# Transposing the attention weights by a product with a diagonal matrix, in the second block of a two-block float32 layer on one core

## The chip, the core and the metric

The kernel runs on one core of a Trainium2 chip. TensorE (PE in the profile) multiplies matrices into PSUM; VectorE (DVE), ScalarE (ACT) and GpSimd (POOL) do the rest of the arithmetic; SyncE (SP) issues most transfers. Each engine works through its own instructions in order and waits on semaphores for the others. The metric is the device time of one execution in microseconds (us), as a median over executions.

## What is computed

The reference runs two blocks on a sequence of 1024 positions of width 1024, all in float32. The first holds a sliding-window attention, an mLSTM, a cross attention and a feed-forward part. The second holds an RWKV-7 recurrence (512 columns) beside a banded attention (8 heads of 64), and an output projection. The change is in the banded attention of the second block:

```python
def chunk_band_attention(q, k, v, q_g, k_g, rel_bias):
    ...
    s = jnp.einsum('bhnqd,bhnkd->bhnqk', qc, kb).astype(jnp.float32) * (HEAD_DIM ** -0.5)
    ...
    s = s + bias[None, :, None]
    s = jnp.where(valid[None, None, :, None, :], s, -1e30)
    p = jax.nn.softmax(s, axis=-1).astype(v.dtype)
    o = jnp.einsum('bhnqk,bhnkd->bhnqd', p, vb)
```

Chunks have 64 rows and see 576 keys (8 chunks to the left and their own). The softmax of each row divides its exponentials by their sum; that division is what the change moves.

## The kernel before

Five programs, one for each engine, are written from one list of steps (class `Order`). Most of the list is made by a planner: `flow` (L666) holds several streams of steps, keeps a clock for each engine, and always takes the next step of the stream that can go on soonest. What a step costs on each engine it reads from the table in `work` (the rows of `band_*` stand at L566 to L576). So a changed cost can change the order in which the engines meet their instructions, and every engine keeps to its order at run time.

The stage around the change begins when the projections of the second block are done, some 2045 us into the span. Four kinds of work run side by side in it:

- preparation of the recurrence's inputs (`prep_*`) for the second half of the sequence, with the row sums at L1898,
- for each of 8 pairs of chunks, the triangular inverse and products of the recurrence (`pre_*`, at L1916 to L2011 on TensorE), a chain of small products in which each level waits for VectorE's copy of the level before (L2808 to L2884),
- the recurrence itself (`seq_*`, L2011 to L2073),
- the banded attention, in units `(j, n)`: a pair of heads j (4 of them) and 128 rows n (8 of them). 32 units run in three lanes (`lane`, L1258), each unit through `band` (L1221).

A unit goes through these steps, for both its heads (a = 0, 1), over W = 128 min(5, n + 1) keys, so that the units with n = 4 to 7, half of them, have the full W = 640:

1. `band_s`: scores, TensorE (L1857); VectorE adds the bias, writes the scores to the buffer `m.Pv3[p]` and takes the maximum (L2699).
2. `band_x`: ScalarE takes the exponential in place, with the row sums as an accumulated output (L3271).
3. `band_p`: VectorE takes the reciprocal of the two columns of sums (L2706), and multiplies each head's 128 x W weights in place by its column (L2710).
4. `band_t`: TensorE transposes the weights, 128 x 128 at a time, by the unit matrix (L1511, the helper `transpose`, which all transposes of the kernel share); ScalarE copies the result out of PSUM (L3279).
5. `band_o`: TensorE multiplies the values by the transposed weights (L1878); `band_y` on VectorE multiplies by the gate (L2716).

When all units with n < 4 and the recurrence are done, the mark "most" lets SyncE fetch what the output projection needs; ScalarE and VectorE split the operand (`fin_part`, L3359 and L2929), then the projection runs on TensorE (`mm`, L1525 to L1527) while the last units end between its products. `mm` splits each float32 product into three products of reduced precision.

The cross attention of the first block (`cross_t`, `cross_o`) is untouched, and is of use for comparison: `cross_t` transposes through the same helper (L1511), and `cross_o` (L1811) is a plain float32 product of 128 x 128 by 128 x 128.

Of the kernel before, what the change touches and what calls it, by code (L numbers as in the profile page):

```python
# [4 lines left out]

F32 = mybir.dt.float32
F32R = mybir.dt.float32r
TOTAL = 52736
ALU = mybir.AluOpType
ACT = mybir.ActivationFunctionType  # L10
AX = mybir.AxisListType
MUL, ADD, SUB, MAX, MIN = ALU.mult, ALU.add, ALU.subtract, ALU.max, ALU.min
# [34 lines left out]
X0 = NCOLS + NROWS + NCST + 32 + NSMALL  # L47
PIECES = [X0, 8192, 2048 * NSLOT, 16384, (TOTAL - X0 - 32768) // 16 * 16]
G0 = X0 + 8192
# [4 lines left out]
class Signals:  # L54
# [12 lines left out]
    def on(self, name, *event, by=1):  # L67
        self.n[name] = self.n.get(name, 0) + by
        assert self.value.setdefault((name, *event), self.n[name]) == self.n[name], (name, event)
        return self.sem(name), by  # L70
# [5 lines left out]
    def at(self, name, *event):  # L76
        assert not self.strict or (name, *event) in self.value, (name, event)
        return self.sem(name), self.value.get((name, *event), 1)
# [58 lines left out]
def v3(ap, k):  # L137
    return ap.rearrange("p (k n) -> p k n", k=k)
# [32 lines left out]
class Memory:  # L171
# [40 lines left out]
    def work(self, a, n):  # L212
        return self.f32(W0 + a, n)
# [18 lines left out]
    def pair(self, b):  # L232
        return self.PS[:, 1024 * b:1024 * b + 1024]
# [27 lines left out]

    def first(self):
        work, f32, small = self.work, self.f32, self.small
        self.xh = [[f32(X0 + 4096 * h + 512 * k, 512) for k in range(8)] for h in range(2)]
        self.xs = [[self.XT[:, k, 512 * h:512 * h + 512] for k in range(8)] for h in range(2)]
        self.aqT, self.akT = v3(work(8192, 4096), 4), work(12288, 1024)
        self.avt = v3(work(13312, 1024), 8)
        self.avf = [work(13312 + 512, 512), work(31784, 512)]
        self.mqk = [work(14336 + 1024 * m, 1024) for m in range(8)]
# [57 lines left out]
    def second(self):  # L327
        work, f32, small = self.work, self.f32, self.small
# [17 lines left out]
        self.pads_s = [work(30720, 513), work(31233, 513)]  # L346
        self.lo, self.hsq = work(31746, 512), work(32258, 512)
        self.mun = small[:, 512:529]
        self.PLc, self.bon = v3(small[:, 544:608], 4), v3(small[:, 608:672], 8)
        m2 = self.m2  # L350
        self.mAR = v3(m2[:, 0:128], 2).unsqueeze(2).to_broadcast([128, 2, 4, 64])
# [207 lines left out]
def work(step):  # L559
# [7 lines left out]
        wide = min(5, x[1] + 1) / 5  # L567
        return [("pe", 1.1 * wide + 0.1), ("v", 1.7 * wide + 0.1)]
    if name == "band_p":
        return [("v", 0.2 + 1.5 * min(5, x[1] + 1) / 5)]  # L570
    if name == "band_x":
        return [("a", 0.2 + 0.85 * min(5, x[1] + 1) / 5)]
    if name == "band_t":
        return [("pe", 0.1 + 0.55 * min(5, x[1] + 1) / 5), ("a", 0.2 + 0.6 * min(5, x[1] + 1) / 5)]
    if name == "band_o":
        return [("pe", 0.1 + 1.1 * min(5, x[1] + 1) / 5)]  # L576
    if name == "rms_out":
# [50 lines left out]
class Order:  # L628
# [206 lines left out]
    def window(self, n, jp):  # L835
        u = 2 * n + jp
        yield from self.after("ha", *[("ws", u - 1)] * (u > 0), ("avt", n // 4))
        yield from self.room((self.pairs, 1), (self.P, 1))
        self.done.add(("ws", u))
        b, free = self.pairs.take()  # L840
        p, pfree = self.P.take()
        st = self.stat()
# [8 lines left out]
        b, free = self.pairs.take()  # L851
        self.P.give(p, ("win.pe", "t", n, jp))
        q, qfree = self.PT.take()
# [92 lines left out]
    def opened(self):  # L946
        ha = ("upto", "pe", "ha")
        for i in range(3):
            self.P.give(i, ha)
        for i in range(2):  # L950
# [9 lines left out]
    def cross(self, n):  # L960
        if n:
            yield from self.after(("cs", n - 1))
        yield from self.after("kv", f"q{n // 4}")
        yield from self.room((self.pairs, 1), (self.P, 1))
        self.done.add(("cs", n))
        b, free = self.pairs.take()
        p, pfree = self.P.take()
        st = self.stat()
# [536 lines left out]
def tensor_program(pe, w, m, S, o):  # L1505

    on, at, bank, pair, cs = S.on, S.at, m.bank, m.pair, m.cs

    def transpose(out, in_):
        n = in_.shape[0]  # L1510
        return pe.transpose(out, in_, m.I[0:n, 0:n])  # L1511
# [349 lines left out]
    def band_t(j, n, a, b, free, p, q, qfree):  # L1861
        w.wait_ge(*at("band.v", "p", j, n, a))
        for e in S.each(free):
            w.wait_ge(*e)
        for kt in range(min(5, n + 1)):
            i = transpose(pair(b)[:, kt * 128:(kt + 1) * 128], m.Pv3[p][:, kt * 128:(kt + 1) * 128])
        i.then_inc(*on("band.pe", "t", j, n, a))

    def band_o(j, n, b, q):
# [220 lines left out]
def vector_program(v, w, m, S, o):  # L2090

    on, at, bank, pair, small = S.on, S.at, m.bank, m.pair, m.small
# [373 lines left out]
    def stats(st, G):  # L2466
        return [small[:, 128 + 32 * st + k * G:128 + 32 * st + (k + 1) * G] for k in range(4)]
# [233 lines left out]
                                   op0=ADD, op1=MIN, accum_out=nm[:, a:a + 1]).then_inc(*on("band.v", "max", j, n, a))  # L2701

    def band_p(j, n, p, st):
        W, sm = 128 * min(5, n + 1), stats(st, 2)[2]
        w.wait_ge(*at("band.a", "x", j, n, 1))
        v.reciprocal(sm, sm).then_inc(*on("band.v", "rcp", j, n))  # L2706
        w.wait_ge(*at("band.v", "rcp", j, n))
        for a in range(2):
            P = m.Pv3[p[a]][:, 0:W]
            v.tensor_scalar(P, P, sm[:, a:a + 1], None, MUL).then_inc(*on("band.v", "p", j, n, a))  # L2710

    def band_y(j, n, b):
        sl = slice(n * 128, (n + 1) * 128)
# [1038 lines left out]
```

## Times and profile before

| What | us |
|---|---|
| median of 3 runs | 2424.62 |
| lowest and highest run | 2422.2 and 2427.26 |
| the profiled execution | 2418.48 |
| its span, first to last instruction | 2416.6 |
| PE busy, share of the span | 2277.8, 94% |
| DVE busy, share of the span | 1456.7, 60% |
| ACT busy, share of the span | 937.6, 39% |
| mean granted clock of TensorE, 1 being 2.4 GHz | 0.972 |

Busy time is the time in which an engine had at least one instruction under way. Matmuls are pipelined, so one of 0.27 us can start 0.11 us after the one before; what a row of matmuls costs is read from the length of a run of them, not from the mean of one. "PEld" is TensorE's loading of weights, which overlaps the products. Idle time is put down to the instruction whose semaphore ended it. The profiled execution ran 6.1 us faster than the median of the runs.

### The profile page before, as it was taken

Reading aid. Unit: us, or ns where it says so; the run is one execution under the profiler, and the core shown is the slowest. Engines: PE = TensorE matmul, PEld = TensorE weight load, DVE = VectorE, ACT = ScalarE, POOL = GpSimd, SP = SyncE. Lnnn points to the kernel's source line nnn. Section 1 sums busy time; section 2 is a strip of 40 time slices with the busy share of each in tenths; the row PEclk is TensorE's granted clock in tenths of the full one; section 3 lists DMA queues with packets and bytes.
Section 4 is the critical chain, followed back from the end, with each engine's and each line's share of the span. In section 5 each row is a group of like instructions: output and inputs, shape, how many; then the busy total and the mean of one; then the engine's idle time right before and its main releaser. Section 6 shows DMA issues by size and latency. Waiting matters only on the chain. (4 is left out here: it accounts for less than half of the span.)

```text
span 2416.6 us, 43216 instructions
## 1 busy us (share of the span) xinstructions
PE 2277.8 (94%) x18830; PEld 1848.8 (77%) x18830; DVE 1456.7 (60%) x2456; ACT 937.6 (39%) x1532; POOL 78.7 (3%) x61
## 2 busy tenths in 40 slices
PE   7999988999999999999999999999999998789789
PEld 5777767788888888888878888778777776567667
DVE  5575866565434886777753454646455655767743
ACT  4446432444333443333342433354333232335441
POOL 0000000000000000000000000002000001200000
PEclk9999989999999999999999999989999999799989
DMA  5332252544123232222365534333323113111044
GB/s 179 88 94 66 69 170 71 173 123 129 53 62 119 77 96 83 79 79 86 93 196 164 157 90 135 98 113 110 109 80 107 51 37 97 41 44 44 3 129 150
DMA packets 329349, 238.15 MB, mean 99 GB/s; under 512 B 10948, under 2 KB 288580, under 8 KB 329032
## 3 DMA queue, kind: packets, MB, share of 16 engines
q1 hardware_dynamic: 326424, 229.82, 31.7%
q10 hardware_dynamic: 2736, 5.57, 0.6%
q8 instruction: 148, 2.42, 0.4%
q14 instruction: 41, 0.34, 0.0%
HBM read 202.33 MB, written 33.03 MB: 97 GB/s over the span
## 5 line engine op out<-in xcount | busy, mean ns | idle before, releaser
L1525 PE MATMUL PS<-SR 128*128 128x512 f32 (+2 forms) x1696 | 681.6, 402 | 43.2 <-DVE SR L2106 34.8
L1526 PE MATMUL PS<-SR 128*128 128x512 f32 (+2 forms) x1696 | 659.9, 389 | 0.0
L1527 PE MATMUL PS<-SR 128*128 128x512 f32 (+2 forms) x1696 | 659.7, 389 | 0.0
L2106 DVE TENSOR_TENSOR SR<-SB,SR 128x1024 fp32r<-128x1024 f32 (+1 forms) x240 | 289.1, 1206 | 289.8 <-ACT SR L2967 289.5
L1525 PEld LDWEIGHTS PS<-SR 128*128 128x128 f32 (+1 forms) x1696 | 320.4, 189 | 128.3 <-DVE SR L2106 36.9
L1527 PEld LDWEIGHTS PS<-SR 128*128 128x128 f32 (+1 forms) x1696 | 320.2, 189 | 68.7
L1526 PEld LDWEIGHTS PS<-SR 128*128 128x128 f32 (+1 forms) x1696 | 320.9, 189 | 62.2 <-issue 1.7
L2967 ACT ACTIVATE SR<-SB 128x1024 fp32r<-128x1024 f32 (+1 forms) x240 | 247.5, 1033 | 254.9 <-DMA SB<-in_w_down 116.1
L1546 PE MATMUL PS<-SR 128*128 128x512 f32 x624 | 243.4, 390 | 0.3 <-DVE SR L2232 0.3
L1548 PE MATMUL PS<-SR 128*128 128x512 f32 x624 | 242.8, 389 | 0.0
L1547 PE MATMUL PS<-SR 128*128 128x512 f32 x624 | 242.7, 389 | 0.0
L1546 PEld LDWEIGHTS PS<-SR 128*128 128x128 f32 x624 | 117.1, 188 | 25.1 <-DVE SR L2232 0.7
L1548 PEld LDWEIGHTS PS<-SR 128*128 128x128 f32 x624 | 117.1, 188 | 24.6
L1547 PEld LDWEIGHTS PS<-SR 128*128 128x128 f32 x624 | 117.1, 188 | 24.4 <-issue 0.2
L1511 PE MATMUL PS<-SB 128*128 128x128 f32 (+2 forms) x560 | 87.1, 288 | 31.9 <-DVE SB L2710 13.5
L1511 PEld LDWEIGHTS PS<-SB 128*128 128x128 f32 (+2 forms) x560 | 63.4, 145 | 49.7 <-DVE SB L2710 15.2
L2974 ACT ACTIVATE SB<-PS 128x512 f32<-128x512 f32 (+1 forms) x71 | 39.1, 572 | 151.1 <-PE PS L1527 113.0
L2254 DVE TENSOR_TENSOR SR<-SB,SR 128x1536 fp32r<-128x1536 f32 (+2 forms) x66 | 87.0, 1347 | 0.9 <-ACT SR L3031 0.9
L3031 ACT ACTIVATE SR<-SB 128x1536 fp32r<-128x1536 f32 (+2 forms) x66 | 74.2, 1156 | 20.0 <-DVE SB L2244 18.9
L2142 DVE TENSOR_TENSOR SB<-PS,SB 128x512 f32<-128x512 f32 x48 | 33.2, 691 | 78.7 <-PE PS L1527 78.7
L3279 ACT ACTIVATE SB<-PS 128x640 f32<-128x640 f32 (+4 forms) x64 | 36.4, 569 | 93.7 <-PE PS L1511 93.6
L3065 ACT ACTIVATE SB<-SB 128x1024 f32<-128x1024 f32 x22 | 27.4, 1245 | 116.5 <-DVE SB L2304 116.5
(315 smaller groups left out, 3032.2 us busy)
## 6 DMA issues: line engine op xcount, KB each, us to landing
SB<-in_w_in SPq DMA_DIRECT2D x110, 512.0 KB, 4.0
SB<-in_w_up SPq DMA_DIRECT2D x88, 256.0 KB, 3.3
SB<-in_w_out SPq DMA_DIRECT2D x32, 512.0 KB, 4.2
SB<-in_w_down SPq DMA_DIRECT2D x32, 512.0 KB, 4.1
SB<-in_w_ada SPq DMA_DIRECT2D x12, 1024.0 KB, 5.2
hidden<-SB SPq DMA_DIRECT2D x22, 512.0 KB, 3.4
SB<-hidden SPq DMA_DIRECT2D x43, 256.0 KB, 5.3
asides<-SB SPq DMA_DIRECT2D x36, 256.0 KB, 4.1
```

Source lines behind the costliest of these rows:

```text
L1511: return pe.transpose(out, in_, m.I[0:n, 0:n])
L1525: pe.matmul(out, whi[:, k - k0, :], hi[k], start=(k == 0), stop=False)
L1526: pe.matmul(out, whi[:, k - k0, :], lo[k], start=False, stop=False)
L1527: i = pe.matmul(out, wlo[:, k - k0, :], hi[k], start=False, stop=(k == j.K - 1))
L1546: pe.matmul(out, whi[:, k, :], hi[k], start=first and k == 0, stop=False, skip_group_check=True)
L1547: pe.matmul(out, whi[:, k, :], lo[k], start=False, stop=False, skip_group_check=True)
L1548: x = pe.matmul(out, wlo[:, k, :], hi[k], start=False, stop=(k == 3), skip_group_check=True)
L2106: v.tensor_tensor(m.f32r(a, kn * cn), m.f32(a, kn * cn), m.f32r(a + 1024, kn * cn).bitcast(F32), SUB).then_inc(*on("split.v", p))
L2254: v.tensor_tensor(m.up_unit(m.SR, p, a, 0, b - a), f32_of(p, a, b - a), m.up_unit(m.SR, p, a, 1, b - a).bitcast(F32), SUB).then_inc(*on("u ...
L2967: a.activation(m.f32r(at_ + 1024, kn * cn), m.f32(at_, kn * cn), ACT.Copy).then_inc(*on("split.a", p))
L2974: a.activation(j.dst(t), src, j.func, scale=j.scale).then_inc(*on("gemm.a", "ev", j.name, t))
L3031: a.activation(m.up_unit(m.SR, p, lo, 1, hi - lo), m.up_unit(m.SB, p, lo, 0, hi - lo), ACT.Copy).then_inc(*on("up.a", "hi", p, g))
```

## The change

The reciprocals are no longer multiplied into the weights. `band_p` multiplies the 128 x 128 unit matrix by the column of reciprocals instead, which gives a diagonal matrix D in a new buffer `m.Dv[p]` (one for each of the five buffers `Pv3`). `band_t` then calls a plain matmul with the unnormalized weights as the stationary operand and D as the moving one, so that the product is the transpose of the weights with each column scaled by its row's reciprocal. The steps, waits and signals stay. The costs in `work` follow: `band_p` from up to 1.7 to 0.6 us on VectorE, `band_t` from up to 0.65 to 1.2 us on TensorE. The piece of memory at the end grows to hold D, and the space set aside for dynamic transfers shrinks.

```diff
-TOTAL = 52736
+TOTAL = 57040
+SCRATCH = 1024
...
+        self.Dv = [work(32816 + 128 * i, 128) for i in range(5)]
...
     if name == "band_p":
-        return [("v", 0.2 + 1.5 * min(5, x[1] + 1) / 5)]
+        return [("v", 0.6)]
...
     if name == "band_t":
-        return [("pe", 0.1 + 0.55 * min(5, x[1] + 1) / 5), ("a", 0.2 + 0.6 * min(5, x[1] + 1) / 5)]
+        return [("pe", 0.1 + 1.1 * min(5, x[1] + 1) / 5), ("a", 0.2 + 0.6 * min(5, x[1] + 1) / 5)]
...
         for kt in range(min(5, n + 1)):
-            i = transpose(pair(b)[:, kt * 128:(kt + 1) * 128], m.Pv3[p][:, kt * 128:(kt + 1) * 128])
+            i = pe.matmul(pair(b)[:, kt * 128:(kt + 1) * 128], m.Pv3[p][:, kt * 128:(kt + 1) * 128], m.Dv[p], start=True, stop=True)
         i.then_inc(*on("band.pe", "t", j, n, a))
...
     def band_p(j, n, p, st):
-        W, sm = 128 * min(5, n + 1), stats(st, 2)[2]
+        sm = stats(st, 2)[2]
         w.wait_ge(*at("band.a", "x", j, n, 1))
         v.reciprocal(sm, sm).then_inc(*on("band.v", "rcp", j, n))
         w.wait_ge(*at("band.v", "rcp", j, n))
         for a in range(2):
-            P = m.Pv3[p[a]][:, 0:W]
-            v.tensor_scalar(P, P, sm[:, a:a + 1], None, MUL).then_inc(*on("band.v", "p", j, n, a))
+            v.tensor_scalar(m.Dv[p[a]], m.I, sm[:, a:a + 1], None, MUL).then_inc(*on("band.v", "p", j, n, a))
...
-    nc = _bacc.Bacc("TRN2", target_bir_lowering=False, num_devices=1)
+    nc = _bacc.Bacc("TRN2", target_bir_lowering=False, num_devices=1, dynamic_dma_scratch_size=SCRATCH)
```

Nothing moves before the first unit of the attention, and SyncE's and GpSimd's instructions keep their order throughout. On the other engines the planner's new costs move instructions at two places of interest. (After the change the same code has a line number 2 higher, and 1 higher behind `band_p`.)

VectorE, at the first units with full width. Before, two scalings of 128 x 640 stand between the recurrence's steps L2835, L2841 and L2847:

```order
L2835 TENSOR_TENSOR SB<-SB 128x512
L2706 RECIPROCAL SB<-SB 128x2
L2710 TENSOR_SCALAR SB<-SB 128x640 x2
L2841 TENSOR_TENSOR SB<-SB 128x512
L2716 SCALAR_TENSOR_TENSOR SB<-PS,SB 128x128
L2706 RECIPROCAL SB<-SB 128x2
L2710 TENSOR_SCALAR SB<-SB 128x640 x2
L2847 TENSOR_TENSOR SB<-PS,SB 128x2x128 x2
```

With the change:

```order
L2836 TENSOR_TENSOR SB<-SB 128x512
L2842 TENSOR_TENSOR SB<-SB 128x512
L2848 TENSOR_TENSOR SB<-PS,SB 128x2x128 x2
L2717 SCALAR_TENSOR_TENSOR SB<-PS,SB 128x128
L2708 RECIPROCAL SB<-SB 128x2
L2711 TENSOR_SCALAR SB<-SB 128x128 x2
L2856 TENSOR_TENSOR SB<-PS,SB 128x2x128 x2
```

The scalings are 128 x 128 now, and the recurrence's steps come ahead of them.

TensorE, at the end of the stage, where the output projection (L1525 to L1527) begins. Before:

```order
L1857 MATMUL PS<-SB 128x512 x2
L1857 MATMUL PS<-SB 128x128 x2
L2073 MATMUL PS<-SB 64x64 x16
L1511 MATMUL PS<-SB 128x128 x5
L1525 MATMUL PS<-SR 128x512
L1526 MATMUL PS<-SR 128x512
L1527 MATMUL PS<-SR 128x512
```

With the change, at the same place and then behind 42 products of the projection (a second such pair of rows follows 12 products later):

```order
L1868 MATMUL PS<-SB 128x128 x10
L1880 MATMUL PS<-SB 64x128 x10
L2075 MATMUL PS<-SB 64x64 x16
L1868 MATMUL PS<-SB 128x128 x5
L1527 MATMUL PS<-SR 128x512
L1528 MATMUL PS<-SR 128x512
```

```order
L1529 MATMUL PS<-SR 128x512
L1859 MATMUL PS<-SB 128x512 x2
L1859 MATMUL PS<-SB 128x128 x2
L1527 MATMUL PS<-SR 128x512
L1528 MATMUL PS<-SR 128x512
```

The scores of the last two units have moved from ahead of the projection into it. Four groups of transposes and three of `band_o` stand behind its first product in both.

## Rows read from the trace of the kernel before

**Rows 1.** The page: busy time of the two busiest engines, its share, instructions.
```profile
PE 2277.8 (94%) x18830; PEld 1848.8 (77%) x18830; DVE 1456.7 (60%) x2456; ACT 937.6 (39%) x1532; POOL 78.7 (3%) x61
```

**Rows 2.** Windows of the stage: length, busy times, granted clock, DMA share, GB/s.
```profile
core 0: us, PE busy (x) PEld busy (x) DVE busy (x) ACT busy (x) POOL busy (x), PEclk, DMA share, GB/s
2045.00:2080.00 35.00, 18.77 (x88) 12.44 (x92) 24.53 (x52) 10.17 (x27) 14.51 (x10) 0.50 0.42 143
2080.00:2120.00 40.00, 34.81 (x956) 28.80 (x952) 27.22 (x79) 16.57 (x37) 0.00 (x0) 0.97 0.05 15
2120.00:2160.00 40.00, 33.12 (x820) 25.77 (x810) 27.78 (x76) 17.03 (x40) 4.70 (x4) 0.87 0.13 47
2160.00:2200.00 40.00, 35.01 (x980) 29.26 (x976) 30.17 (x82) 15.57 (x31) 0.97 (x1) 1.00 0.19 66
2200.00:2240.00 40.00, 35.89 (x931) 27.31 (x931) 27.93 (x95) 18.09 (x53) 3.50 (x4) 0.99 0.04 10
2240.00:2280.00 40.00, 34.31 (x843) 27.54 (x840) 31.34 (x83) 16.56 (x31) 4.97 (x4) 0.96 0.01 3
2280.00:2317.00 37.00, 20.07 (x259) 14.89 (x255) 21.89 (x52) 19.91 (x36) 4.46 (x4) 0.78 0.16 41
2317.00:2341.00 24.00, 23.30 (x147) 18.59 (x147) 10.09 (x15) 8.54 (x13) 0.00 (x0) 0.91 0.57 180
sum 296.00, PE 235.29 PEld 184.60 DVE 200.94 ACT 122.44 POOL 33.11; mean PE 29.41 PEld 23.07 DVE 25.12 ACT 15.31 POOL 4.14
```

**Rows 3.** Chain that ended last, 2045 to 2341 us: shares by engine and line.
```profile
by line: PE PS L1857 9.8%; PE PS L1878 9.3%; PE PS L1511 8.7%; DVE SB L2699 5.9%; issue 5.5%; PE PS L1946 5.3%; DVE SB L2710 4.6%; PE PS L1999 2.8%; ACT SB L3279 2.3%; PE PS L1916 2.2%; PE PS L1984 2.2%; PE PS L1525 2.2%; PE PS L1527 1.8%; 
```

**Rows 4.** Waits of PE, 2080 to 2341 us: total us, times, longest.
```profile
PE PS L1525 <- DVE SR L2106: 9.2, 1, 9.2
PE PS L1511 <- DVE SB L2699: 6.1, 8, 2.8
PE PS L1857 <- ACT SB L3279: 5.5, 6, 1.6
PE PS L1511 <- DVE SB L2710: 5.3, 5, 4.1
```

**Rows 5.** Groups by line and shape, 2040 to 2360 us: the transposes of the stage.
```profile
L1511 PE MATMUL PS<-SB 128*128 128x128 f32 x240 | 42.3, 299 | 22.0 <-DVE SB L2710 13.5 <-DVE SB L2699 6.1 <-ACT SB L3279 2.1
```

**Rows 6.** Timeline of the cross attention at full clock: start, length, engine, line.
```profile
626.42 3.73 PE L1811 MATMUL PS<-SB 128*128 128x128 f32 x32
...
629.99 1.04 PE L1511 MATMUL PS<-SB 128*128 128x128 f32 x8
```

**Rows 7.** L2710 alone, windows of the stage, their sum.
```profile
sum 296.00, DVE 31.80; mean DVE 3.98
```

**Rows 8.** Timeline: pairs of L2710, narrow, beside GpSimd's work, and wide.
```profile
2052.26 0.48 DVE L2710 TENSOR_SCALAR SB<-SB 128x128 f32<-128x128 f32 x2
...
2151.54 2.57 DVE L2710 TENSOR_SCALAR SB<-SB 128x512 f32<-128x512 f32 x2
2152.68 1.15 POOL L3401 TENSOR_TENSOR SB<-SB 128x512 f32<-128x512 f32 x1
...
2309.22 1.02 DVE L2710 TENSOR_SCALAR SB<-SB 128x640 f32<-128x640 f32 x2
```

**Rows 9.** Timeline: scores of a full unit at half and at full clock.
```profile
2295.73 2.50 PE L1857 MATMUL PS<-SB 64*128 64x512 f32 x8 [1.65 <-ACT SB L3279]
...
2305.47 1.35 PE L1857 MATMUL PS<-SB 64*128 64x512 f32 x8 [0.79 <-ACT SB L3279]
```

**Rows 10.** Timeline up to the start of the output projection.
```profile
2307.62 0.82 DVE L2699 CUSTOM_DVE_ANT_0 SB<-PS,SB 128x640 f32<-128x640 f32 x1
...
2310.94 4.27 ACT L3359 ACTIVATE SR<-SB 128x512 fp32r<-128x512 f32 x8 [0.86 <-ACT SB L3271]
...
2317.70 0.80 PE L1525 MATMUL PS<-SR 128*128 128x512 f32 x1 [9.17 <-DVE SR L2106]
```

## The prediction

> **What bounds the kernel now.** I read the page first, then the stage of the change in windows, then the chain of waits in it, and last single rows for prices. The page gives TensorE 94% of the span and VectorE 60% [rows 1], but the change touches only the 296 us from 2045 to 2341, so the windows decide. There TensorE is busy for 235.3 us and VectorE for 200.9 [rows 2]; both are loaded. In the 200 us from 2080 to 2280 TensorE is busy for 173.1 us, 87%, and VectorE for 144.4, 72%. In the last 24 us TensorE has next to no gap: the output projection fills it. Only at both ends is it short of work: 18.8 of 35 us before 2080, where VectorE prepares the recurrence, and 20.1 of 37 us from 2280 to 2317, where little is left but attention units that wait for themselves.
>
> The chain of waits says whether these 13% of gaps mean that TensorE is free. It is not: the three largest shares of the chain are the attention's own products, scores 9.8%, values 9.3%, transposes 8.7%, and VectorE's scaling L2710 has 4.6% [rows 3]. TensorE's waits are many and short; after the one for the projection's weights (9.2 us, once) the longest sums are 5 to 6 us each [rows 4]. The engines hand each other a dense chain, and TensorE has the greater part of it.
>
> **The change, part by part.**
>
> *TensorE, transposes become products.* The stage has 240 of them: 30 pieces for each of 8 heads, and 240 records in the group [rows 5], one for each. The price of a transpose: 8 back to back take 1.04 us; less the tail of the last (0.27), that is 0.77 / 7 = 0.11 us each [rows 6]. The price of a float32 product of the same shape: in the cross attention 16 of L1811 stand as 32 records, 3.73 us together, so (3.73 - 0.27) / 31 = 0.112 us a record and 0.223 us a product [rows 6]. The new product has the same stationary 128 x 128 and moving 128 x 128, so it should run as two records. Added: 240 x 0.112 = 26.9 us at full clock, twice that at half clock. A group of five goes from 0.72 to 1.28 us.
>
> A rule of the Trainium skill speaks against this edit. Perfetto Trace Analysis, section Transposes, says to use a transpose wherever one is meant, not a standard matmul, since transposes skip the arithmetic. The trace agrees in sign, with 0.11 against 0.223 us. FP8 and Floating Point Precision, section TensorE Precision Notes, goes further: true float32 takes four passes. By that the added time would be three passes, 240 x 3 x 0.112 = 81 us. The trace has two records for a product of this shape, and I take what it has.
>
> How much of 26.9 us lies on the path? The chain holds 8.7% of 296 us = 25.8 of the 42.3 us of transposes, 61%. So 0.61 x 26.9 = 16.4 us come in directly. Of the other 10.5 us, hidden behind VectorE now, I let 4 come in, somewhat over a third: TensorE has 27 us of gaps in the busy 200, in many pieces below the 0.56 us that a group grows by. For half clock (windows at 0.87 and 0.78) I add 1.5 us.
>
> *VectorE, wide scalings become narrow.* 64 scalings are busy for 31.8 us [rows 7]. A pair of 128 x 128 takes 0.48 us, of 128 x 640 1.02 us [rows 8], so 64 x 0.24 = 15.4 us remain and 16.4 us go. Some of that is a clash: a pair of 128 x 512 takes 2.57 us while GpSimd works [rows 8]. On the path are 4.6% of 296 = 13.6 us; by the same ratio (15.4 / 31.8) 7.0 us of it go. The rest, 9.4 us, lies beside TensorE's work and brings nothing directly; it is why I let under half of the hidden transposes come in. If this cover were gone, it would be worth up to those 9.4 us. The reads of the unit matrix cost what the reads of a 128 x 128 piece cost now.
>
> *ScalarE* does what it did. Its copy L3279 starts when a group of transposes ends, now 0.56 us later, and the exponential of the next unit is queued behind it, then that unit's reciprocal on VectorE. That is the knock-on effect in the share of the path above, not a further term.
>
> *The order.* The scores of two full units move from ahead of the projection into it. Ahead of it, in the stretch that waits for itself, a unit's scores are 1.35 us at full or 2.50 at half clock [rows 9], and VectorE's maximum follows with 0.82 us for each head before the rest [rows 10]. The last pair ahead of the mark goes, and with it about 1.35 + 2 x 0.8 = 3 us, and part of the pair before: I take 4 us. Behind the projection's start TensorE is full, so the same scores cost 2 x 1.35 = 2.7 us there. Net -1.3 us. The bounds are 0 and -6 (both pairs gone at half clock, 2 x (2.5 + 1.6) = 8.2, less 2.7). The projection's first wait of 9.2 us [rows 4], for the operand's split (from 2310.94 to 2317.70 [rows 10]), stays as long as it is, since ScalarE's and VectorE's work in it is the same.
>
> *The rest.* The new buffers and the memory set aside move no instruction of SyncE or GpSimd: 0. No wait is added; what stood behind `band_p` and `band_t` still does.
>
> **Sum**: 16.4 + 4 + 1.5 - 7.0 - 1.3 = **+13.6 us** on the profiled execution's 2418.5 (span 2416.6 and 1.9 around it), so 2432.1. The median of the runs before is 2424.6, 6.1 above the profiled execution; the same step on it gives **2438.2 us**. A measurement of this kernel can tell about 0.2%, 4.8 us, from no change.
>
> **The rivals.**
>
> *TensorE is the bound and nothing hides.* All 26.9 us come in, 1.5 for the clock, and VectorE's relief is worth nothing, since it only waits longer. For it: 87% against 72% busy. Against it: a third of the chain is on VectorE and ScalarE. It gives 26.9 + 1.5 - 1.3 = +27, 2452 us. Chance 0.17.
>
> *VectorE decides, and the kernel gets faster.* Mechanism: in the stage's middle TensorE's filler is placed in gaps that it would spend waiting for VectorE's steps of the recurrence. If these come 0.54 us sooner for each full unit, and the longer transposes fit into the gaps, the path loses the 7.0 us of L2710 and what the clash with GpSimd makes of it, some 2 us more, and 1.3 for the order, and gains the products only where nothing covers them: the 20 transposes within the projection, 2.2 us. That is -8, 2416.5 us. It decides where the gap ahead of a group is at least 0.56 us. For it: TensorE idles 61 us in the stage, and its waits for L2710 and L2699 are 11.4 us from 2080 on [rows 4]. Against it: 61% of the transposes are on the path already. Chance 0.15.
>
> *The clock gives it back.* The granted clock is 0.78 from 2280 to 2317 and 0.87 from 2120 to 2160 [rows 2], stretches in which TensorE has gaps or waits for a pair of scalings. With 0.78, 44% of the time is at the 1.2 GHz level, so of 20.1 us of work 0.44 x 20.1 / 2 = 4.4 us would go at 2.4 GHz; with 0.87, 0.26 x 33.1 / 2 = 4.3 us; the windows at 0.96, 0.97 and 0.91 hold 1.4, 1.0 and 2.1 more. If more work on TensorE keeps it at the upper level, up to 13 us come back, and the sum is near 0: 2425 us. It bears on this that 0.50 was granted before 2080 with TensorE busy half of the time. TensorE: Matmul & The Clock Gate, Part 4, says that transposes don't count as activity for the clock as products do, which would favour this rival. The trace neither shows nor refutes it: the transposes stand among products throughout. Chance 0.12.
>
> *Float32 costs four passes here.* The change would then add twice the work again, about +70 us, 2495 us; the rows of L1811 speak against it. Chance 0.03.
>
> **How the numbers follow.** The forecast itself, with bounds of its terms (4 to 10 for what was hidden, -4 to -9 for VectorE, 0 to -6 for the order) from 2430 to 2446, has 0.53. The range takes in most of the first two rivals and the third: 2419 to 2452 us; outside it lie the upper half of the first rival, part of the second, and the fourth, together about 0.2. Slower by over 0.2%: 0.53 + 0.17 + 0.03 = 0.73, of which 0.02 lie near the bound, 0.71. Within: 0.14. Faster: 0.15.
>
> **What the profile would show.** Right: the transposes' line with 480 records for 240 products, 60 to 70 us busy; L2710's heir at 15 to 18 us; TensorE above 90% busy from 2080 on, the projection starting some 12 us later; the three attention products leading the chain, with the transposes first. Wrong: 240 records, or 960; TensorE's busy share unchanged with longer waits for ScalarE's copies; a granted clock of 1.0 up to the projection; or a stage that ends before 2341, with waits on VectorE gone.

## The result and the profile after

| | before | after |
|---|---|---|
| median of the runs, us | 2423.91 (4 runs) | 2436.08 (4 runs) |
| lowest and highest | 2422.2 and 2427.26 | 2433.98 and 2437.85 |
| the profiled execution | 2418.48 | 2433.98 |
| its span | 2416.6 | 2432.2 |

The ratio is 1.0054, with a 95% interval of 1.0040 to 1.0067: 13.1 us slower (9.7 to 16.2); the medians differ by 12.2 us. The forecast was 13.6 us on the median of before, 2438.2.

The first line of the page after, against [rows 1]:

```profile
PE 2305.8 (95%) x19070; PEld 1882.4 (77%) x19070; DVE 1443.6 (59%) x2456; ACT 937.6 (39%) x1532; POOL 78.2 (3%) x61
```

TensorE has 240 instructions and 28.0 us of busy time more, VectorE 13.1 us less, ScalarE the same. The windows of the stage after, with the columns of [rows 2] and one window more, since the stage is longer:

```profile
2045.00:2080.00 35.00, 22.20 (x144) 16.41 (x148) 24.30 (x53) 8.79 (x24) 12.90 (x8) 0.52 0.37 133
2080.00:2120.00 40.00, 35.72 (x874) 30.33 (x865) 22.94 (x67) 14.02 (x30) 0.00 (x0) 0.96 0.01 3
2120.00:2160.00 40.00, 35.40 (x878) 28.84 (x876) 26.62 (x81) 16.32 (x40) 4.46 (x4) 0.91 0.19 59
2160.00:2200.00 40.00, 37.85 (x922) 32.57 (x920) 23.90 (x68) 16.38 (x34) 0.00 (x0) 1.00 0.20 66
2200.00:2240.00 40.00, 38.90 (x954) 32.10 (x950) 26.97 (x98) 17.57 (x48) 4.83 (x4) 1.00 0.03 10
2240.00:2280.00 40.00, 33.48 (x853) 27.94 (x854) 28.85 (x82) 14.12 (x29) 4.52 (x4) 1.00 0.01 3
2280.00:2317.00 37.00, 29.99 (x387) 25.60 (x386) 14.96 (x43) 16.21 (x30) 4.46 (x4) 0.82 0.01 2
2317.00:2341.00 24.00, 16.24 (x129) 12.76 (x129) 10.89 (x17) 9.78 (x15) 0.00 (x0) 0.86 0.69 208
2341.00:2357.00 16.00, 16.00 (x85) 12.55 (x86) 9.98 (x20) 7.62 (x14) 0.00 (x0) 1.00 0.34 99
```

From 2080 to 2280 TensorE is busy for 181.4 of 200 us, 91% where it was 87%; VectorE fell from 72% to 65%. The chain over the stage after, against [rows 3], leads with the new products:

```profile
by line: PE PS L1868 18.6%; PE PS L1859 10.5%; PE PS L1880 8.0%; PE PS L1948 6.4%; DVE SB L2701 4.2%; issue 3.7%; PE PS L1934 3.3%; PE PS L2001 3.1%; PE PS L1527 2.6%; PE PS L1529 2.3%; PE PS L1528 2.3%; PE PS L1986 2.3%; PE PS L1918 2.1%; 
```

L1868, the product by D, has 18.6% of 312 us = 58 us of the chain, where the transposes had 26; the scalings are gone from the list. The group by shape, against [rows 5], and one group of five, from the timeline inside the projection at full clock:

```profile
L1868 PE MATMUL PS<-SB 128*128 128x128 f32 x480 | 76.1, 306 | 19.7 <-DVE SB L2711 13.4 <-DVE SB L2701 4.1 <-ACT SB L3280 2.0
```

```profile
2353.31 1.27 PE L1868 MATMUL PS<-SB 128*128 128x128 f32 x10
```

There are 480 records for 240 products. In this group ten records take 1.27 us, (1.27 - 0.27) / 9 = 0.111 us a record, the price of [rows 6]. Most full-clock groups of five products within the stage take 1.38 us, where most groups of five transposes took 0.77: 0.61 us more, against the 0.56 of the prediction. The rows, before and after:

```profile
2104.05 0.77 PE L1511 MATMUL PS<-SB 128*128 128x128 f32 x5
```

```profile
2105.87 1.38 PE L1868 MATMUL PS<-SB 128*128 128x128 f32 x10
```

The waits of TensorE from 2080 us on, against [rows 4] (total us, times, longest):

```profile
PE PS L1527 <- DVE SR L2108: 7.8, 1, 7.8
PE PS L1868 <- DVE SB L2711: 5.4, 2, 4.3
PE PS L2001 <- DVE SB L2848: 4.7, 6, 1.6
PE PS L1868 <- DVE SB L2701: 4.1, 3, 2.1
...
PE PS L1859 <- ACT SB L3280: 1.0, 2, 0.8
```

The scores L1859 hardly wait for ScalarE's copies now (1.0 us for 5.5), and the waits on VectorE are about as before: what TensorE lost, it did not lose in a new wait.

The scalings after, the sum over windows up to 2360 us against [rows 7], and a narrow pair that clashes with GpSimd:

```profile
sum 315.00, DVE 18.89; mean DVE 2.10
```

```profile
2063.90 2.13 DVE L2711 TENSOR_SCALAR SB<-SB 128x128 f32<-128x128 f32 x2
```

18.9 us are left of 31.8, a saving of 12.9 us and not 16.4. Nearly all narrow pairs take 0.48 us; some stand beside GpSimd's work, and there a narrow pair is hardly cheaper than a wide one (2.13 us here, 2.23 for 128 x 256 before).

**A ruler for the experiments.** The first scores of the stage start at 2049.5 us before and at 2046.9 after, though the instructions ahead of them are the same; over all kernels below that start lies between 2046.3 and 2053.6. So I cut each profiled execution there and at the first product of the projection. Part A is from the first scores to the projection, part B from there to the end. The row of part A before, and the one after:

```profile
2049.50:2317.70 268.20, 211.99 (x4833) 166.01 (x4833) 191.50 (x513) 113.06 (x251) 31.60 (x24) 0.88 0.13 42
```

```profile
2046.90:2328.20 281.30, 237.00 (x5036) 196.70 (x5036) 175.53 (x502) 111.02 (x245) 31.17 (x24) 0.89 0.13 40
```

Part A grows by 13.1 us, part B by 5.1 (98.9 to 104.0). Part B's start and the two scores that moved into it:

```profile
2328.22 0.79 PE L1527 MATMUL PS<-SR 128*128 128x512 f32 x1 [7.76 <-DVE SR L2108]
...
2340.82 1.35 PE L1859 MATMUL PS<-SB 64*128 64x512 f32 x8
...
2345.07 1.35 PE L1859 MATMUL PS<-SB 64*128 64x512 f32 x8
```

The 5.1 us of part B are the two moved scores (2 x 1.35) and 20 products, 20 x 0.112 = 2.2. Part A has 220 products, 24.6 us more work, and grew by little over half of that. The two parts together grew by 18.2 us, 5 more than the 13.1 of the runs. A part is read from one execution of each kernel; over all kernels below, the difference of A + B lies between 2 us under and 5 us over that of the runs. So the parts tell where time went, and how much only to a few us. The experiments ask what gave the rest back: VectorE's relief, the gaps, or the order.

### The profile page after: what moved, and what is told of

It reads as the page before. It is cut to its first block and busy times, and to the rows that moved or that the text cites. A ratio compares the mean times of both kernels' runs of the same rounds, so it can differ in the third digit from the quotient of the medians.

```text
span 2432.2 us, 43704 instructions
## 1 busy us (share of the span) xinstructions
PE 2305.8 (95%) x19070; PEld 1882.4 (77%) x19070; DVE 1443.6 (59%) x2456; ACT 937.6 (39%) x1532; POOL 78.2 (3%) x61
## 5 line engine op out<-in xcount | busy, mean ns | idle before, releaser
L1527 PE MATMUL PS<-SR 128*128 128x512 f32 (+2 forms) x1696 | 682.2, 402 | 40.7 <-DVE SR L2108 32.4
L1527 PEld LDWEIGHTS PS<-SR 128*128 128x128 f32 (+1 forms) x1696 | 320.7, 189 | 125.6 <-DVE SR L2108 34.3
L1549 PEld LDWEIGHTS PS<-SR 128*128 128x128 f32 x624 | 117.2, 188 | 24.6 <-issue 0.2
L1868 PE MATMUL PS<-SB 128*128 128x128 f32 x480 | 76.1, 306 | 19.7 <-DVE SB L2711 13.4
L1868 PEld LDWEIGHTS PS<-SB 128*128 128x128 f32 x480 | 64.5, 208 | 28.5 <-DVE SB L2711 14.6
L3032 ACT ACTIVATE SR<-SB 128x1536 fp32r<-128x1536 f32 (+2 forms) x66 | 74.1, 1155 | 19.9 <-DVE SB L2246 18.8
L2312 DVE SCALAR_TENSOR_TENSOR SB<-SB 128x1024 f32<-128x1024 f32 x44 | 56.5, 1285 | 26.5 <-ACT SB L3066 25.7
```

Source lines behind the costliest of these rows:

```text
L1527: pe.matmul(out, whi[:, k - k0, :], hi[k], start=(k == 0), stop=False)
L1549: pe.matmul(out, whi[:, k, :], lo[k], start=False, stop=False, skip_group_check=True)
L1868: i = pe.matmul(pair(b)[:, kt * 128:(kt + 1) * 128], m.Pv3[p][:, kt * 128:(kt + 1) * 128], m.Dv[p], start=True, stop=True)
L2312: v.scalar_tensor_tensor(out=O, in0=v3(m.padg[:, i:i + 1024], 2), scalar=m.col("fw", 3 * p + i), in1=O, op0=MUL, op1=ADD).then_inc(*on("up ...
L3032: a.activation(m.up_unit(m.SR, p, lo, 1, hi - lo), m.up_unit(m.SB, p, lo, 0, hi - lo), ACT.Copy).then_inc(*on("up.a", "hi", p, g))
```

## The experiments

Each is compared with runs of before on the same chip; differences are the ratio less 1, times the median of before, with its 95% interval. The twelve kernels were run in three sets of four on three chips, and the change's own difference is that of its first measurement.

### Taking the change apart, with the order held

First the change with the planner's two old costs, which restores the order of before on every engine:

```diff
     if name == "band_p":
-        return [("v", 0.6)]
+        return [("v", 0.2 + 1.5 * min(5, x[1] + 1) / 5)]
...
     if name == "band_t":
-        return [("pe", 0.1 + 1.1 * min(5, x[1] + 1) / 5), ("a", 0.2 + 0.6 * min(5, x[1] + 1) / 5)]
+        return [("pe", 0.1 + 0.55 * min(5, x[1] + 1) / 5), ("a", 0.2 + 0.6 * min(5, x[1] + 1) / 5)]
```

> The change with the planner's old costs, so that every engine meets its instructions in the order of before: products by D and narrow scalings, nothing moved. The mixed theory (most of the added product time comes in, about half of the scalings' time goes, the order is worth 1.3 us) expects +14.9 us against before, and so 1 to 2 us more than the change itself. If TensorE were the bound everywhere: +28. If the new order is worth 4 us or more, this kernel is at +16 or above; if the new order does harm, it is below the change's own +12.2.

Then the opposite, the kernel before with the two new costs and nothing else.

> Before with the planner's new costs: wide scalings and true transposes in the new order. The mixed theory expects -1.3 us, with the projection starting some 4 us sooner and 2.7 us of scores moved behind its start. If the order of before was fitted to its costs, and an order planned for other costs leaves holes, +3 us or more.

Then the two halves of the work alone, both in the old order. Narrow scalings with true transposes (D is computed, and not used):

```diff
-            i = pe.matmul(pair(b)[:, kt * 128:(kt + 1) * 128], m.Pv3[p][:, kt * 128:(kt + 1) * 128], m.Dv[p], start=True, stop=True)
+            i = transpose(pair(b)[:, kt * 128:(kt + 1) * 128], m.Pv3[p][:, kt * 128:(kt + 1) * 128])
```

> Old order, narrow scalings of the unit matrix, but true transposes by the unit matrix: the weights stay undivided by their sums, so part of the computation is left out. It prices VectorE's relief alone. The mixed theory expects -7 us. If VectorE decides in the middle of the stage: -9 or more. If TensorE is the bound and VectorE's time is only waiting: 0 to -2.

And wide scalings with products by the unit matrix:

```diff
-            i = transpose(pair(b)[:, kt * 128:(kt + 1) * 128], m.Pv3[p][:, kt * 128:(kt + 1) * 128])
+            i = pe.matmul(pair(b)[:, kt * 128:(kt + 1) * 128], m.Pv3[p][:, kt * 128:(kt + 1) * 128], m.I, start=True, stop=True)
```

> Old order, wide scalings as before, transposes made as float32 products by the unit matrix: it prices TensorE's addition alone. The mixed theory expects +22 us (16.4 on the path, 4 of the hidden, 1.5 for the clock). If TensorE is the bound: +28. If the products mostly fill gaps: +10 or less. The sum of this and the kernel with narrow scalings only should be that with both in the old order, within 3 us, if the two effects don't interact; if narrow scalings are worth something only when TensorE is short of work, the sum of the two parts is lower than the whole.

| kernel | transposes | scalings | order | difference, us | part A | part B |
|---|---|---|---|---|---|---|
| before | true | wide | old | | 268.2 | 98.9 |
| narrow only | true | narrow | old | -4.4 (-6.8 to -1.9) | 265.1 | 99.4 |
| product only | product | wide | old | +23.0 (+19.6 to +26.4) | 291.8 | 101.5 |
| both, old order | product | narrow | old | +19.6 (+16.5 to +22.8) | 288.7 | 101.3 |
| the change | product | narrow | new | +13.1 (+9.7 to +16.2) | 281.3 | 104.0 |
| new order alone | true | wide | new | +1.0 (-1.2 to +3.1) | 267.8 | 103.0 |

The two halves add up: 23.0 - 4.4 = 18.6 against 19.6 together. In part A it is 23.6 - 3.1 = 20.5 against 20.5. Agreement this close is partly luck, since each difference of the runs is known to some 3 us. VectorE's relief is worth -4.4 us beside transposes and 19.6 - 23.0 = -3.4 beside products, about the same, and the rival by which it decides the stage, which needed -9 or more, falls. The rows of part A for the product alone and for narrow scalings alone:

```profile
2051.50:2343.30 291.80, 241.09 (x5052) 199.00 (x5052) 191.09 (x513) 112.91 (x251) 31.57 (x24) 0.88 0.12 39
```

```profile
2046.50:2311.60 265.10, 210.91 (x4832) 164.96 (x4832) 180.16 (x513) 112.70 (x250) 31.30 (x24) 0.89 0.13 43
```

The chain of the product alone over its part A:

```profile
by line: PE PS L1866 19.1%; PE PS L1857 10.3%; PE PS L1878 8.9%; PE PS L1946 6.1%; issue 5.1%; DVE SB L2699 4.7%; DVE SB L2710 3.9%; ACT SB L3279 3.8%; PE PS L1932 2.7%; PE PS L1984 2.7%; PE PS L1999 2.1%; PE PS L1916 1.8%; DVE SR L2929 1.7
```

The products L1866 hold 19.1% of it, 56 of their 70.8 us of busy time in this part, 79%, where the transposes had 61%. With products alone TensorE is busy for 29.1 us more and part A is 23.6 us longer: only 5.5 of its 56.2 us of gaps are filled. With narrow scalings alone VectorE works 11.3 us less and part A is 3.1 us shorter.

These rows bear on the clock too. In one and the same order the granted clock of part A is 0.88 with transposes and 0.88 with products, in spite of 29 us more work on TensorE. So the rival by which more work on TensorE brings the upper level, and with it the loss, falls. The Trainium skill, TensorE: Matmul & The Clock Gate, Part 4, says that transposes do not count for the clock as products do. The trace does not bear it out here: swapping 220 of the one for 220 of the other, amid much other work, moved the share by nothing that its two digits show. What an order does to the clock is another matter, and comes below.

The last two rows of the table are what I had not foreseen. The new order alone changes nothing for the old work, but with the new work it takes 7.4 us from part A (288.7 to 281.3) for 2.7 more in part B: 4.7 us net in the profiled executions, 6.5 by the runs (19.6 less 13.1, each known to some 3 us).

### What the order is worth, and whether by fit or by luck

The change with only one of the two new costs:

> The change with the planner's new cost for band_t on TensorE and the old one for band_p on VectorE. The change in the old order came out at +19.6 us, the change itself at +12.2, so the new order is worth some 7 us to the new work. If that is because the planner leaves longer gaps for the longer products, nearly all of it stands here: +12 to +14. If it knows VectorE's relief that matters, this one stays at +18 to +20.

> The change with the planner's new cost for band_p alone, the old one for band_t. If the cost of the products is what the order needs: +18 to +20, as in the old order. If VectorE's cost is: +12 to +14. If orders differ by luck, by several us whatever the costs, this kernel and the one with band_t's cost alone come out anywhere, 10 to 22.

The change twice, and then the kernel before, each with one number of the planner's table changed whose work the edit leaves alone:

```diff
-        "band_y": [("v", 0.28)],
+        "band_y": [("v", 0.32)],
```

> The change itself, with one unrelated number of the planner's table changed a little, band_y from 0.28 to 0.32 us, which moves some 150 rows on TensorE and leaves all work as it is. It shows how far two orders planned for the same work differ by chance. If the fit of the costs is what counts: +12.2, within 2. If chance plays a part as large as the 7 us: 4 us or more away from it.

```diff
-"pre_up": [("pe", 0.67), ("v", 0.84)],
+"pre_up": [("pe", 0.67), ("v", 0.88)],
```

> The change itself with another unrelated number changed a little (pre_up from 0.84 to 0.88 us on VectorE), which moves some 100 rows on TensorE. With the first such number it was at +19.9 where the change is at +12.2. If the change's own order is a lucky one among orders planned with right costs: +16 to +22. If the first was an unlucky one: +11 to +14.

```diff
     if name == "band_x":
-        return [("a", 0.2 + 0.85 * min(5, x[1] + 1) / 5)]
+        return [("a", 0.2 + 0.92 * min(5, x[1] + 1) / 5)]
```

> Before with one number of the planner's table changed a little (band_x from 0.85 to 0.92 us on ScalarE), which moves some 150 rows on TensorE: the scatter of orders for the old work. For the new work five orders came out between +10.9 and +27.4 us. If the scatter belongs to the planner: 3 us or more away from 0, on either side. If TensorE's shorter transposes leave room that absorbs it: within 2 us of 0, as the order of the change did with the old work (+1.0).

| work | order planned with | difference, us | A + B |
|---|---|---|---|
| new | both new costs (the change) | +13.1 (+9.7 to +16.2) | 385.3 |
| new | both, and pre_up changed | +12.6 (+8.5 to +16.5) | 380.6 |
| new | both, and band_y changed | +19.9 (+16.5 to +23.2) | 389.2 |
| new | band_t's new cost alone | +10.9 (+7.5 to +14.3) | 378.8 |
| new | band_p's new cost alone | +27.4 (+23.7 to +31.0) | 392.4 |
| new | both old costs | +19.6 (+16.5 to +22.8) | 390.0 |
| old | old costs | | 367.1 |
| old | both new costs | +1.0 (-1.2 to +3.1) | 370.8 |
| old | band_x changed | +1.2 (-1.5 to +4.1) | 369.5 |

Both answers are partly right. The cost of the products is the one that matters: with it alone the kernel is where the change is (+10.9 and +13.1), and with VectorE's relief told to the planner but the products still booked as transposes it is the worst of all, 27.4 us slower. But one of three orders planned with right costs is 7 us worse than the other two, by a change of 0.04 us in one number. So of the gain of the change's order over the old one (6.5 us) a part may be chance, and from these runs it cannot be said how much. For the old work three orders lie within 1.2 us of each other. That the shorter transposes leave room which absorbs a less fitting order is what I had offered for this case; it fits, and three orders don't prove it.

The windows show two things by which these orders differ. First the part A with band_t's new cost alone, then parts A and B with band_y changed:

```profile
2051.00:2326.00 275.00, 231.91 (x5034) 192.14 (x5034) 179.55 (x505) 111.55 (x247) 31.21 (x24) 0.92 0.13 41
```

```profile
2046.30:2322.70 276.40, 224.48 (x4977) 186.76 (x4977) 175.24 (x496) 106.36 (x235) 31.15 (x24) 0.91 0.13 41
2322.70:2435.50 112.80, 108.04 (x560) 88.07 (x560) 41.94 (x63) 30.11 (x44) 0.00 (x0) 0.98 0.43 134
```

One is the clock. The granted clock of part A is 0.88 for the new work in the old order, 0.89 in the change's, and 0.91 to 0.92 in the two with one number changed and in the one with band_t's cost alone. That last one has as many TensorE records in part A as the change (5034 and 5036), but keeps TensorE busy for 231.9 us instead of 237.0: 5.1 us of the 6.3 by which its part A is shorter. The clock of the whole span shows it in every run, and not only in the profiled ones: 0.969 to 0.971 for the new work in the old order and 0.967 to 0.971 with band_p's new cost alone, 0.971 to 0.973 for the change, 0.971 to 0.975 with band_t's cost alone, 0.973 to 0.976 with one number changed. So a part of what an order is worth is the clock that it is granted, though more work in one order moved nothing (0.969 to 0.972 for the product alone, 0.968 to 0.972 for the runs of before beside it); what in an order brings it no run separates. The other is the place of the work. The order that came out 7 us worse has a short part A (276.4 us) at a good clock, and loses in part B: 112.8 us where the change has 104.0, with 60 more records (560 and 500) behind the projection's start.

### Where a product's price comes from

Old order, narrow scalings, and the product in the float32 type of reduced precision (`m.PvR` and `m.DvR` are views of `m.Pv3` and `m.Dv` in that type; the exponential and the scaling write through them, which rounds the weights and D; of the edit only the product is shown):

```diff
-            i = pe.matmul(pair(b)[:, kt * 128:(kt + 1) * 128], m.Pv3[p][:, kt * 128:(kt + 1) * 128], m.Dv[p], start=True, stop=True)
+            i = pe.matmul(pair(b)[:, kt * 128:(kt + 1) * 128], m.PvR[p][:, kt * 128:(kt + 1) * 128], m.DvR[p], start=True, stop=True)
```

> Old order, narrow scalings, and the product by D with weights and D in the float32 type of reduced precision that the projections use, which takes one record where full float32 takes two (so the weights are rounded when they are written). If what costs is the second record, a group of five is about 0.7 us as a transpose is, and this equals narrow scalings with true transposes, -4.4 us (-2 to -7). If a product costs more than a transpose for another reason, such as the loading of its weights (0.19 against 0.14 us), it is at +3 or above.

It came out at -0.5 us (-2.9 to +1.9), so 20 us below the float32 product in the same order, and 4 above narrow scalings with true transposes. Its usual group of five pieces, and ten pieces of two groups; behind them the same ten pieces as transposes in the kernel before:

```profile
2104.59 0.77 PE L1870 MATMUL PS<-SR 128*128 128x128 f32 x5
```

```profile
2100.36 1.52 PE L1870 MATMUL PS<-SR 128*128 128x128 f32 x10 [0.30 <-DVE SB L2703]
```

```profile
2099.83 1.51 PE L1511 MATMUL PS<-SB 128*128 128x128 f32 x10 [0.30 <-DVE SB L2699]
```

There is one record for each product, and a group costs what a group of transposes costs: 0.77 us for five of either, 1.52 and 1.51 us for ten. So the whole of the product's added price is its second record, and the slower loading of weights that the expectation offered as the other cause (0.19 against 0.14 us) does not show in the length of a group. The 4 us that are left against true transposes are not in the price of a piece. The two intervals overlap (-2.9 to +1.9 and -6.8 to -1.9), and the granted clock of part A was 0.87 here and 0.89 there; whether the 4 us are real is open.

### A way to relieve VectorE without TensorE

ScalarE is the least loaded of the three. In the kernel before, it scales the second head's weights in VectorE's place (ScalarE's side of the edit; VectorE keeps the first head's scaling, and the second head's transposes wait for ScalarE):

```diff
...
+    def band_p(j, n, p, st):
+        P, sm = m.Pv3[p[1]][:, 0:128 * min(5, n + 1)], stats(st, 2)[2]
+        w.wait_ge(*at("band.v", "rcp", j, n))
+        a.activation(P, P, ACT.Copy, scale=sm[:, 1:2]).then_inc(*on("band.a", "p", j, n))
...
```

> Before, in its own order, with the second head's weights scaled by ScalarE (a copy with the column of reciprocals as scale) instead of VectorE: half of VectorE's scaling time goes, some 16 us, with no time added on TensorE. It leaves nothing of the result out. Narrow scalings with true transposes took the same 16 us from VectorE and gained 4.4 us. If VectorE's load is what that gained from: -2 to -4, less what ScalarE's longer way (0.8 against 0.5 us, behind its queue) costs. If the wait of a unit for its own scaling counts more than the load: 0 to +4.

It is 12.3 us slower (7.7 to 16.9), far outside both expectations. Waits of its part A, longest first:

```profile
ACT SB L3283 <- PE PS L1511: 57.7, 32, 5.1
DVE SB L2699 <- PE PS L1857: 41.3, 24, 6.4
ACT SB L3276 <- DVE SB L2706: 41.2, 22, 8.9
...
PE PS L1857 <- ACT SB L3283: 13.2, 10, 3.9
```

L3276 is the new scaling. It waits 41.2 us for the reciprocals L2706 (22 times, up to 8.9 us), and behind it in ScalarE's queue stand the copies L3283 that free PSUM for the next scores; TensorE's scores wait 13.2 us for them, where they waited 5.5 before [rows 4]. I take the wait to be what costs, and not ScalarE's added work. If so, an order that knows of the step must mend it:

```diff
     if name == "band_p":
-        return [("v", 0.2 + 1.5 * min(5, x[1] + 1) / 5)]
+        return [("v", 0.2 + 0.75 * min(5, x[1] + 1) / 5), ("a", 0.2 + 0.6 * min(5, x[1] + 1) / 5)]
```

> The same, with the planner's costs for band_p fitted to it, which moves about 160 rows on TensorE. If a fitted order is worth several us: 2 to 5 us below the one in the old order. If orders scatter: within +-6 us of it, on either side.

It came out at -3.1 us (-6.1 to -0.5): 15 us below the same work in the old order, far beyond both expectations (5 and 6 us). Its waits shrank as the account asks:

```profile
ACT SB L3276 <- DVE SB L2706: 28.4, 19, 4.5
...
PE PS L1857 <- ACT SB L3283: 6.8, 7, 2.8
```

ScalarE's work is the same in both, so it is not what cost 12.3 us; that the wait is the whole of it is not shown, since an order changes much else. It is the only kernel with the whole computation in full precision that came out below before. The interval just excludes no change, and an order's luck is of the same size, so I call it promising and no more.

## Why the prediction was right, and where it was not

**TensorE's addition.** 240 x 0.112 = 26.9 us at full clock; measured 28.0 us of busy time over the whole kernel, two records a product, 0.111 us each. The rival by which a product costs four transposes (0.03) falls, with the 81 us. The rule from which I took it does not fall with it. The Trainium skill, FP8 and Floating Point Precision, section TensorE Precision Notes, gives true float32 four passes. Rows of the kernel before agree, where a product of 128 x 512 in float32 (L1589) stands among products of the same shape in the reduced type:

```profile
811.22 0.39 PE L1547 MATMUL PS<-SR 128*128 128x512 f32 x1
811.44 0.40 PE L1548 MATMUL PS<-SR 128*128 128x512 f32 x1
811.67 1.02 PE L1589 MATMUL PS<-SB 128*128 128x512 f32 x2
812.13 0.79 PE L1546 MATMUL PS<-SR 128*128 128x512 f32 x1
812.76 0.39 PE L1547 MATMUL PS<-SR 128*128 128x512 f32 x1
```

Products in the reduced type follow each other after 0.23 us. The float32 product and one in the reduced type take 812.76 - 811.67 = 1.09 us, so the float32 one takes 0.86, in two records: 3.8 times as much. What was wrong was to count a transpose as one of the four passes. At 128 columns a transpose costs half of the float32 product (0.11 and 0.22 us), and the reduced type's product costs what a transpose costs. The Trainium skill's rule in Perfetto Trace Analysis, section Transposes (a transpose and not a product), holds for float32 with 0.11 against 0.22 us; for the reduced type it brought nothing, 0.77 us for five of either.

**How much of it comes in.** The sum had 16.4 + 4 + 1.5 = 21.9 us; with all else held it is 23.0 (19.6 to 26.4). The share was about right: 16.4 + 4 is 76% of 26.9, and measured are 23.6 of 29.1 us in part A, 81%, or by the runs 23.0 of the 31.6 us by which TensorE is busier in both parts, 73%. But it was put together from the transposes' 61% of the chain and a guess of 4 us, and which hidden transposes became last no run shows. The clock's term was too small. Part A's 220 products are 24.6 us at full clock and TensorE is busy for 29.1 us more; at a granted clock of 0.88 a quarter of the time is at half clock, which by my estimate is 0.24 x 24.6 = 5.9 us, where the sum had 1.5.

**VectorE's relief.** The sum had -7.0; measured alone it is -4.4 (-6.8 to -1.9). The price was wrong: I let 16.4 us go on VectorE at the narrow pair's 0.48 us, and 12.9 went, since the pairs beside GpSimd did not get much cheaper. Of those, 4.4 us came in, 34% and not the chain's 43%; the interval (15 to 53%) doesn't tell the two apart.

**The order.** The sum had -1.3, from 4 us at the end of part A less 2.7 in part B. Part B was right (+5.1 with 2.2 for its products). The 4 us at the end of part A are not there: from the last product of the recurrence's second step (L2042, start 2285.7 before, 2292.6 after) to the projection it takes 32.0 us before and 35.6 after, and with the new work in the old order 35.3. With scores gone from that stretch, groups of five and of ten products at half clock stand in it (here ten, as 20 records in 4.60 us):

```profile
2304.81 2.50 PE L1859 MATMUL PS<-SB 64*128 64x512 f32 x8 [0.79 <-ACT SB L3280]
...
2308.34 4.60 PE L1868 MATMUL PS<-SB 128*128 128x128 f32 x20 [1.03 <-DVE SB L2701]
```

What the order gave, 7.4 us in part A against the old order, lies ahead of that, in the middle: from the first scores to that product it is 253.4 us in the old order and 245.7 in the new. The windows ahead of that product and behind it, old order and then new:

```profile
2051.10:2304.50 253.40, 221.68 (x4883) 184.69 (x4884) 161.47 (x468) 95.15 (x219) 26.83 (x20) 0.91 0.12 38
2304.50:2339.80 35.30, 19.95 (x176) 15.03 (x172) 18.79 (x45) 17.70 (x32) 4.46 (x4) 0.66 0.17 47
```

```profile
2046.90:2292.60 245.70, 216.15 (x4848) 179.75 (x4848) 157.27 (x458) 91.73 (x211) 26.71 (x20) 0.91 0.12 39
2292.60:2328.20 35.60, 20.85 (x196) 16.95 (x190) 18.27 (x44) 19.30 (x34) 4.46 (x4) 0.76 0.17 46
```

The middle has 35 records fewer, and 5.5 us of its 7.7 are less work of TensorE. Of those records 16 are the two moved scores of part B. Another 20 now stand at the end of part A, which takes them in 0.3 us more, at a granted clock of 0.76 where it was 0.66. I had named neither place nor size.

**The sum by the runs**: +23.0 - 4.4 + 1.0 (what the halves miss) - 6.5 (order, net) = +13.1, where the forecast had 21.9 - 7.0 - 1.3 = 13.6. That the total came within 0.5 us is luck: the relief was taken too high by 2.6, the order's gain too low by 5.2, and the products too low by 1.1 and 1.0, each by measurements known to some 3 us. The order's term was the most wrong of them. The bounds that I gave for the terms also add up to 2431.5 to 2448.5 us, and not to the 2430 to 2446 that I wrote.

**The rivals.** *TensorE is the bound*: with 73 to 81% coming in it is the nearest of the four, and had the order stayed as it was the result (19.6) would lie between it and the forecast. *VectorE decides* fell, as said. So did *the clock gives it back* as it stood, by more work on TensorE; by the order the clock did move, from 0.88 in part A to 0.89 with the change and to 0.92 with others. Of the signs listed, the 480 records and the lead of the products in the chain came as told. Four did not quite: the products' line is busy for 76.1 us, over the 60 to 70 stated; VectorE's heir at 18.9 us is over the 15 to 18; TensorE is above 90% busy only up to 2280 us, and from there to 2341 for 46.2 of 61 us, 76%; and the projection starts 10.5 us later and not 12 (13.1 by the ruler).

## What to carry to other kernels

Moving work from a less loaded engine to the most loaded one was paid for the greater part there (23.0 us of 28 to 32) and refunded by about a third (4.4 of 12.9 us), even though both looked loaded: price both directions before the edit. A chain's share gave the size of what comes in and no bound: 61% where 73 to 81% came in, 43% where 34% did. When a planner or a hand-written order stands between the edit and the queues, a changed instruction has to be told to it, the cost that grew above all; and a few orders from irrelevant changes show how far orders scatter, here 7 us on an effect of 13. An instruction that waits for another engine and is put into a queue of work that others need can cost more by its wait than by its length.

## What the runs showed that I had not expected

- A product of 128 x 128 by 128 x 128 in the reduced type, with one record, cost what a float32 transpose of that shape cost: 0.77 us for five, 1.52 and 1.51 us for ten. The float32 product took 1.38 us for five.
- A narrow scaling beside GpSimd's work cost about what a wide one did there: 2.13 us for a pair of 128 x 128, 2.57 for 128 x 512, against 0.48 us for a narrow pair without it and 1.02 us for the widest, 128 x 640.
- 29 us more of TensorE's work in a stretch of 268 left its mean granted clock at 0.88, while another order of the same work moved it from 0.88 to 0.92.
- The same instructions up to the stage reached it at times up to 7 us apart (2046.3 to 2053.6 us) from one profiled execution to the next. A cut at a fixed event takes that out of a comparison of two profiles; a few us of scatter are left.
